# The chunk inverses of an RWKV-7 layer: 64x64 triangles doubled block by block, or two 32x32 diagonal blocks and a correction between them

## What is computed

```python
def step(S, inp):
    rt, wt, kt, vt, at, bt = inp
    sa = jnp.einsum('bhvk,bhk->bhv', S, at)
    S = S * wt[:, :, None, :] + sa[..., None] * bt[:, :, None, :] + vt[..., None] * kt[:, :, None, :]
    return S, jnp.einsum('bhvk,bhk->bhv', S, rt)
```

## Time and profile before

| | |
|---|---|
| three timed runs | 1850.35, 1838.9, 1853.22 us |
| span of the profiled execution | 1837.3 us |
| time of the profiled execution around its span | not given by the profile |
| the block's inverses, first mask of XT to last addition | 366.69 to 413.24 us |
| TensorE, VectorE, ScalarE busy over the span | 1732.0, 640.1, 345.0 us |

### The profile page before, as it was taken

One profiled execution on the slowest core, in us unless ns is written; L12 is line 12 of the kernel. 1 busy time (PEld: TensorE's weight loads), 2 busy tenths in 40 slices (PEclk: granted clock), 3 DMA queues, 4 the chain that ended last, 5 costly groups with the idle time before them and its releaser, 6 DMA issues.

```text
span 1837.3 us, 41974 instructions
## 1 busy us (share of the span) xinstructions
PE 1732.0 (94%) x19056; PEld 1137.2 (62%) x19056; DVE 640.1 (35%) x1196; ACT 345.0 (19%) x558; POOL 39.7 (2%) x49
## 2 busy tenths in 40 slices
PE   6989898789899999998999999999999999999994
PEld 6967565589899999996934435344353534447342
DVE  5534443674865544855632010120101002010021
ACT  3223231402443333534210000000000000000001
POOL 0010000000000000000000000000000000010100
PEclk9999999698999999999999999999999999999998
DMA  9130540200854443517499999999999999997995
GB/s 292 52 112 1 150 141 20 38 3 4 240 161 151 150 137 105 170 62 230 172 386 414 418 413 418 415 417 417 410 417 403 417 415 406 417 398 306 415 405 220
DMA packets 171303, 474.02 MB, mean 258 GB/s; under 512 B 28426, under 2 KB 114604, under 8 KB 140228
## 3 DMA queue, kind: packets, MB, share of 16 engines
q1 hardware_dynamic: 168574, 461.05, 66.3%
q0 software_dynamic: 2352, 10.23, 1.6%
q10 hardware_dynamic: 198, 0.05, 0.0%
HBM read 459.19 MB, written 15.24 MB: 258 GB/s over the span
## 4 chain that ended last, share of the span: by engine, by line
PE 47%; SPq 3%; DMA 2%; DVE 1%; issue 1%; ACT 0%; POOL 0%; POOLq 0%; ACTq 0%; DVEq 0%
PE bank L2662 43%; SPq L2321 2%; DMA ring<-in_moe_w_down 1%; PE bank L319 1%; PE bank L320 1%; PE bank L321 1%; SPq L2431 0%; SPq L2325 0%; PE bank L2513 0%; PE bank L2592 0%; PE bank L2636 0%; DMA ring<-y_rows_dram,y_index 0%; PE bank L2528 0%; PE bank L2547 0%; PE bank L2630 0%
## 5 line engine op out<-in xcount | busy, mean ns | idle before, releaser
L2662 PE MATMUL bank<-ring,x 128*32 128x512 f32 (+1 forms) x6144 | 587.3, 540 | 2.3 <-DMA ring<-in_moe_w_gu 2.0
L2662 PEld LDWEIGHTS bank<-ring,x 128*32 128x32 f32 x6144 | 203.9, 110 | 354.4 <-issue 333.7
L2662 PE MATMUL bank<-ring,hid 128*32 128x256 f32 x5376 | 292.1, 379 | 0.3 <-DMA ring<-in_moe_w_down 0.3
L2662 PEld LDWEIGHTS bank<-ring,hid 128*32 128x32 f32 x5376 | 184.4, 110 | 108.1 <-issue 2.3
L319 PE MATMUL bank<-x_hi,w_hi 128*128 128x320 f32 (+1 forms) x488 | 151.8, 311 | 0.0
L320 PE MATMUL bank<-x_lo,w_hi 128*128 128x320 f32 (+1 forms) x488 | 150.8, 309 | 0.0
L321 PE MATMUL bank<-x_hi,w_lo 128*128 128x320 f32 (+1 forms) x488 | 150.8, 309 | 0.0
L2130 DVE TENSOR_TENSOR w_lo<-ring,w_hi 128x2048 fp32r<-128x2048 f32 (+2 forms) x51 | 112.5, 2209 | 97.5 <-ACT w_hi L2052 97.2
L3015 DVE TENSOR_TENSOR hrow<-sil,bank 128x512 f32<-128x512 f32 (+1 forms) x48 | 26.9, 617 | 301.3 <-PE bank L2662 301.3
L2052 ACT ACTIVATE w_hi<-ring 128x2048 fp32r<-128x2048 f32 (+2 forms) x51 | 94.1, 1848 | 126.8 <-PE bank L321 124.2
L2787 ACT ACTIVATE sil<-bank 128x512 f32<-128x512 f32 (+1 forms) x48 | 22.7, 544 | 455.2 <-PE bank L2662 455.2
(11 more groups left out here) (576 smaller groups left out, 2122.8 us busy)
## 6 DMA issues: line engine op xcount, KB each, us to landing
ring<-in_moe_w_gu SPq DMA_DIRECT2D x128, 1024.0 KB
ring<-in_moe_w_down SPq DMA_DIRECT2D x112, 1024.0 KB
ring<-in_moe_w_gu SPq DMA_DIRECT2D x128, 768.0 KB
ring<-in_ffn_w_gu_even SPq DMA_DIRECT2D x44, 512.0 KB, 4.9
pages<-in_cache_mla SPq DMA_DIRECT2D x128, 144.0 KB, 2.5
ring<-in_w_in_odd SPq DMA_DIRECT2D x12, 1024.0 KB, 5.3
ring<-in_ffn_w_down_even SPq DMA_DIRECT2D x10, 1024.0 KB, 5.4
proj_ring<-in_w_in_even SPq DMA_DIRECT2D x9, 1024.0 KB
```

The lines of the kernel that those rows point to most:

```text
L2662: mm = t.matmul(ps[banks[g3]][SL * y:SL * y + SL, 0:w], act[:, g3, k, :], m_ring[:, slot, at + y * w:at + (y + 1) * w], start=start, stop= ...
```

## The change

The two diagonal 32x32 blocks of each 64x64 triangle are inverted first, in compact form, and the block that couples them comes in at the end:

- X, T1 and a new `XT_blocks` (XTb) are [128, 3, 8, 32]: the rows of a 32-row block hold that block's own 32 columns. `begin` takes them out of BM: rows of even blocks from columns 0 to 31, those of odd blocks from 32 to 63, by two masks and an addition. It has five operations where it had three.
- The levels 2 to 16 go through the same steps with 32x32 blocks: `level` has four matmuls per head on tiles 0 and 1 and two on tile 2, each 32 rows by 32 columns with 32 moving columns, in the four diagonal 32x32 tiles of the array. VectorE's operations have 256 elements for 512. Tile 2 leaves out its last update of X as before.
- Level 32 is replaced: a product of BM's off-diagonal block with X of the even blocks, which lands on the rows of the odd blocks; a copy into T1; a product of T1 and XTb, which lands on the rows of the even blocks; and an operation that adds this, on the even rows alone, to the right half of XT (`scalar_tensor_tensor`). Two products and two VectorE operations per tile, as before, but 16 matmuls each.
- ScalarE spreads XTb into the full XT: two activations per tile with a scale that is 1 on the rows of even or odd blocks and 0 elsewhere.
- The table of constants has 3804 columns for 3962.

```diff
--- before.py
+++ after.py
@@ -75,9 +75,13 @@
     s8T[:64, 64:128] = ((il // DS == jl // DS) & (il <= jl))[:64]
     f["sm_T"] = s8T
     f["ident64"] = il == jl
-    for s in (2, 4, 8, 16, 32):
-        f[f"lev{s}"] = (il // (2 * s) == jl // (2 * s)) & (il % (2 * s) >= s) & (jl % (2 * s) < s)
-    f["lev1_T"] = (il // 2 == jl // 2) & (jl % 2 >= 1) & (il % 2 < 1)
+    ib, jb = i % 32, p[None, 0:32]
+    for s in (2, 4, 8, 16):
+        f[f"lev{s}"] = (ib // (2 * s) == jb // (2 * s)) & (ib % (2 * s) >= s) & (jb % (2 * s) < s)
+    f["even32"], f["odd32"] = i // 32 % 2 == 0, i // 32 % 2 == 1
+    for half in ("even32", "odd32"):
+        f["lev1_" + half] = (ib // 2 == jb // 2) & (jb % 2 >= 1) & (ib % 2 < 1) & f[half]
+    f["ident32"] = ib == jb
     f["causal"] = np.where(i >= j, 0.0, -1e30)
 
     f["own"] = np.where((i % DS >= np.arange(DS)[None, :]), 0.0, -1e30)
@@ -1214,15 +1218,15 @@
                     KM = sbuf(rk, "KM", [P, 3, RH, 2, RC])
                     XT = sbuf(rk, "XT", [P, 3, RH, RC])
                     inv = rk.enter_context(ExitStack())
-                    X = sbuf(inv, "X", [P, 3, RH, RC])
-                    T1 = sbuf(inv, "T1", [P, 3, RH, RC])
+                    X, XTb, T1 = (sbuf(inv, n, [P, 3, RH, 32]) for n in ("X", "XT_blocks", "T1"))
                     pairs_full, pairs_ready, keys_full, keys_ready, xt_ready = (sem(x) for x in ("pairs_full", "pairs_ready", "keys_full", "keys_ready", "xt_ready"))
                     t_full, t_ready, d_full, d_ready = ([sem(f"{x}{i}") for i in range(3)] for x in ("t_full", "t_ready", "d_full", "d_ready"))
-                    LEVELS = [[2, 4, 8, 16, 32], [2, 4, 8, 16, 32], [2, 4]]
+                    LEVELS = [[2, 4, 8, 16], [2, 4, 8, 16], [2, 4]]
                     BLOCKS = [2, 2, 1]
+                    xt_spread = sem("xt_spread")
 
                     def heads(bank, r=P):
-                        return ps[bank][0:r, :].rearrange("p (h t) -> p h t", h=RH)
+                        return ps[bank][0:r, 0:RH * 32].rearrange("p (h t) -> p h t", h=RH)
                     ROWS = [rowB[:, 0, :], rowB[:, 1, :], rowK[:, 0, :], rowK[:, 1, :], rowB[:, 2, :]]
                     with nc.Block() as block:
                         @block.sync
@@ -1312,20 +1316,22 @@
                                 last.then_inc(ready, 1)
 
                             def over(name, r):
-                                return C(name, r).rearrange("p (o t) -> p o t", o=1).to_broadcast([r, RH, RC])
+                                return C(name, r).rearrange("p (o t) -> p o t", o=1).to_broadcast([r, RH, 32])
                             def begin(i):
                                 r = TILES[i][1]
                                 v.wait_ge(pairs_full, i + 1)
                                 masked(BM, i, (2 * i, 2 * i + 1), pairs_ready)
                                 v.wait_ge(pairs_ready, i + 1)
-                                dv(v, v.tensor_tensor(XT[0:r, i, :, :], BM[0:r, i, :, 0, :], over("lev1_T", r), ALU.mult))
-                                dv(v, v.tensor_tensor(XT[0:r, i, :, :], XT[0:r, i, :, :], over("ident64", r), ALU.add))
-                                v.transpose(X[0:r, i, :, :].rearrange("p h t -> p (h t)"), XT[0:r, i, :, :].rearrange("p h t -> p (h t)")).then_inc(xt_ready, 1)
+                                v.tensor_tensor(XTb[0:r, i, :, :], BM[0:r, i, :, 0, 0:32], over("lev1_even32", r), ALU.mult)
+                                dv(v, v.tensor_tensor(T1[0:r, i, :, :], BM[0:r, i, :, 0, 32:64], over("lev1_odd32", r), ALU.mult))
+                                dv(v, v.tensor_tensor(XTb[0:r, i, :, :], XTb[0:r, i, :, :], T1[0:r, i, :, :], ALU.add))
+                                dv(v, v.tensor_tensor(XTb[0:r, i, :, :], XTb[0:r, i, :, :], over("ident32", r), ALU.add))
+                                v.transpose(X[0:r, i, :, :].rearrange("p h t -> p (h t)"), XTb[0:r, i, :, :].rearrange("p h t -> p (h t)")).then_inc(xt_ready, 1)
                             v.wait_ge(st_full, NB)
                             v.wait_ge(stored.sem, stored.n)
                             begin(0)
                             begin(1)
-                            for li in range(5):
+                            for li in range(4):
                                 tiles = [i for i in range(3) if li < len(LEVELS[i])]
                                 for i in tiles:
                                     r = TILES[i][1]
@@ -1343,9 +1349,17 @@
                                         v.wait_ge(d_ready[i], li)
                                     else:
                                         v.wait_ge(xt_ready, i + 1)
-                                    if li < len(LEVELS[i]) - 1:
+                                    if i < 2 or li == 0:
                                         v.tensor_tensor(X[0:r, i, :, :], X[0:r, i, :, :], heads(2 * i + 1, r), ALU.add)
-                                    v.tensor_tensor(XT[0:r, i, :, :], XT[0:r, i, :, :], heads(2 * i, r), ALU.add).then_inc(d_ready[i], 1)
+                                    v.tensor_tensor(XTb[0:r, i, :, :], XTb[0:r, i, :, :], heads(2 * i, r), ALU.add).then_inc(d_ready[i], 1)
+                            for i in range(2):
+                                v.wait_ge(t_full[i], 5)
+                                v.tensor_copy(T1[:, i, :, :], heads(2 * i)).then_inc(t_ready[i], 1)
+                            for i in range(2):
+                                v.wait_ge(d_full[i], 5)
+                                v.wait_ge(xt_spread, i + 2)
+                                v.scalar_tensor_tensor(out=XT[:, i, :, 32:64], in0=heads(2 * i + 1), scalar=C("even32"), in1=XT[:, i, :, 32:64],
+                                                       op0=ALU.mult, op1=ALU.add).then_inc(d_ready[i], 1)
 
                         @block.scalar
                         def _(s):
@@ -1383,6 +1397,11 @@
                             for n in range(5):
                                 s.wait_ge(row_full, n + 1)
                                 s.activation(ROWS[n], ps[6 + n % 2][:, :], ACT.Copy).then_inc(row_act, 1)
+                            for i in (2, 0, 1):
+                                r = TILES[i][1]
+                                s.wait_ge(d_ready[i], len(LEVELS[i]))
+                                s.activation(XT[0:r, i, :, 0:32], XTb[0:r, i, :, :], ACT.Copy, scale=C("even32", r))
+                                s.activation(XT[0:r, i, :, 32:64], XTb[0:r, i, :, :], ACT.Copy, scale=C("odd32", r)).then_inc(xt_spread, 1)
 
                         @block.tensor
                         def _(t):
@@ -1455,11 +1474,16 @@
                                                           src[hs, pr, js], AR[hs, pr, :, js], start=True, stop=True)
                                 return mm
 
+                            def rows32(b):
+                                return slice(32 * b, 32 * b + 32)
+
+                            def cols32(h):
+                                return slice(32 * h, 32 * h + 32)
+
                             def level(i, bank, left, right):
                                 for h in range(RH):
-                                    for b in range(BLOCKS[i]):
-                                        js = slice(RC * b, RC * b + RC)
-                                        mm = t.matmul(ps[bank][js, h * RC:(h + 1) * RC], left(h, js), right(h, js), start=True, stop=True)
+                                    for b in range(2 * BLOCKS[i]):
+                                        mm = t.matmul(ps[bank][rows32(b), cols32(h)], left(h, b), right(h, rows32(b)), start=True, stop=True)
                                 return mm
 
                             t.wait_ge(ar_ready, 1)
@@ -1480,22 +1504,34 @@
                                         for q in range(2):
                                             mm = t.matmul(ps[6][64 * q:64 * q + 64, cols], bks[:, q, c, :], C("ident"), start=True, stop=True, tile_position=(0, 64 * q))
                                 mm.then_inc(row_full, 1)
-                            for li in range(5):
+                            for li in range(4):
                                 tiles = [i for i in range(3) if li < len(LEVELS[i])]
                                 for i in tiles:
                                     if li:
                                         t.wait_ge(d_ready[i], li)
                                     else:
                                         t.wait_ge(xt_ready, i + 1)
-                                    level(i, 2 * i, lambda h, js: BM[js, i, h, 0, :], lambda h, js: X[js, i, h, :]).then_inc(t_full[i], 1)
+                                    level(i, 2 * i, lambda h, b: BM[rows32(b), i, h, 0, cols32(b % 2)], lambda h, js: X[js, i, h, :]).then_inc(t_full[i], 1)
                                 if li < 3:
                                     t.wait_ge(*((keys_ready, li) if li else (row_act, 5)))
```

(18 more changed lines are left out.)

## The result

The changed kernel takes 1866.25 us, the median of 11 runs (1854.3 to 1873.61), against 1849.1 us for the kernel before in the same comparison (11 runs, 1837.89 to 1853.22). The ratio is 1.0103, 95% interval 1.0079 to 1.0126: slower by 1.0%, 14.6 to 23.3 us. The forecast was 1837.

The account below looks back on a forecast made before the run. TensorE was taken as the bound, with the block's gain reaching the end one to one. Level gains of 12.8 us and up to 0.2 for constants made 13, so 1850.35 - 13 = 1837 us; range 1827 to 1855.

Parts of the forecast that it names:

- What bounds the kernel, and that the block's length reaches the end: Whole kernel: TensorE, busy 94%, is the bound; no transfer sets the block's end, so its gain reaches the end one to one.
- The sum: Whole kernel: level gains of 12.8 us plus 0 to 0.2 for constants make 13, subtracted from the median 1850.35: 1837.
- A product's cost: Block's levels: a four-tile product of 64 pairs costs between 0.50 and 1.87 us, taken as 0.55; before, products were 0.93 apart.
- The 29 ns of before: Stretches longer than 2 us show no pair quicker than 29 ns, taken as the tiles' limit, not the supply's.
- My 31 ns for a record of 32x32: New products: from 110 and 58 ns for records 64 columns apart, 32 columns come to about 31 ns.
- Rival 2: TensorE's supply is worse than 19 ns a pair; at 29 ns the block ends 18 us later, 1868 us; chance 0.11.
- The clock: Block of the changed kernel: granted clock expected at 0.9 or more.
- rival 3: The clock falls as four 32x32 blocks half fill the array; levels 4 to 32 3 us slower, 1854 us; chance 0.13.
- VectorE: Block: operations on 256 elements take 0.41 us, each masking or update saves 0.27, a tile's start takes 2.0 us.
- The levels: Levels 2, 4, 8, 16, 32 gain 3.6, 2.6, 2.0, 2.6, 2.0 us; block 33.7 instead of 46.6, level 32 3.4.
- What a switch between tile shapes costs: Around the keys' pairs TensorE changes between 64-row and 32-row tiles six times, 0.2 us each, 1.2 in all.

Follow-up runs that it names:

- the last kernel: Kernel before with X by VectorE's transposition up to level 16, level 32 as off-diagonal products, keys' pairs ahead of tile 2's product: 1840.6 us, ratio 0.9969.
- half the count: Changed kernel with one matmul of 64 columns for two heads, using the first head's weights, so fewer pairs on the same tiles: 1845.2 us, ratio 0.9978.
- the wide left operands: Kernel with block-diagonal left operands in 64 columns, compact right operands with 32 columns moving, X by transposition, 64-row tiles: 1846.2 us, ratio 0.9985 to before.
- a kernel that doesn't stall: Kernel before with only the change's level 32, two off-diagonal products in 32-row tiles: 1846.4 us, ratio 0.9996.
- the halves: Kernel before with each 64x64 product matmul issued as two of 32 columns, same tiles and sums: 1925.5 us, ratio 1.0374.
- the transposition: X made by VectorE's 32x32 transposition instead of a product and an addition: in the changed kernel 1845.3 us, in the kernel before (up to level 16) 1845.2 us.

## Why the prediction was wrong

**What bounds the kernel, and that the block's length reaches the end: held.** 13.6 and 14.3 us more in the block, 17 us more in the median; 65 more gave 69, 76 more gave 76, 8 less gave 6 (the last kernel) and 5 (half the count), 5 less gave 2 (the wide left operands). The differences are within what the spread of the runs hides, and I leave them open. The sum was rightly taken from the median: the profiled execution of before was one of those that kept the full clock from 120 to 160 us. But "So no transfer is under way whose landing could set the end of the block" overlooked one kind: the 1% of load in the block was, by the view of transfers from 366.69 to 413.24 us, nothing but 10 packets of instructions, 9 of them on queue 8.

**A product's cost: this step failed.** "So a four-tile product costs between 0.50 and 64 x 29 ns = 1.87 us. I take 0.55, near the rows 439 and 1626, where tiles change as they will here." In a burst that was right: 8 ns a pair at 418.35. But those rows hold 45 and 4 matmuls, and a portion of instructions holds 128. Within a portion a row shows how fast TensorE reads what is there; only beyond it does it show how fast more arrives. From stall to stall a pair costs 28.5 ns (ten portions, 36.5 us), so a product of 64 costs 1.8 us, at my upper bound and more than three times my 0.55; over the whole block, with its waits, it is 30.9 ns, and 1950 pairs make 60.2 us. The rows bounded another quantity than the one that I needed. I had written that supply at no cost "is shown for 1 us only" and gave it a chance of 0.55 all the same.

**The 29 ns of before were read wrongly as well.** I took them for the time of 64 columns ("there the tiles set it"). With 32 columns they are 29 ns too, and they double with the clock, so the tile does set them but the moving columns don't. My 31 ns for a record of 32x32 came out of a difference of columns on 64-row tiles and agreed with the 8 ns a pair on four 32-row tiles by luck. That the supply's 28.5 ns lie so near these 29 hid the limit: the kernel before drew pairs about as fast as they can come, without one wait for issue among its products.

**The rival.** Rival 2 named the mechanism (supply worse than 19 ns a pair), with the decisive remark that the program holds twice the matmuls, and its far end, 29 ns, gave 1868 for the 1866.25 measured; its block end, 18 us later, was 4 too late, since the switches and short waits that I added (3.2 us) lie inside the stalls. That 1868 came so near is in part luck: the median rose by 3 us more than the block. It had a chance of 0.11 and lay outside the range. The bounds of the unknown cost were 0.50 and 1.87 us, and the range should have reached to what the upper one gives. By the 25 ns of the Trainium skill ("TensorE: Matmul & The Clock Gate", "Wait — 56ns, not 53.3ns?") the end would come 11 us later, near the truth, but not by its rule: starts are 8 to 14 ns apart here on four tiles and 1.7 us at the stalls. Gotcha 1 of the Trainium skill's "TensorEngine Tiling (Array Packing)", by which row tiles can't use one bank at the same time, doesn't hold here either: four row tiles write one bank at those 8 ns a pair.

**The clock.** I expected 0.9 or more, and it was 0.64. With the same tiles, 64 columns moving and half the count it stays at 0.90, so the half filled array of rival 3 doesn't bring it down by itself; of the kernels with 32-row tiles those that stall more have the lower clock (0.90, 0.73, 0.64, 0.54 for 4, 11, 18 and 40 us before issue). Which is the cause of which is not shown. It cost nothing that shows in the block, since a pair cost 31 ns at 0.54 as at 0.73.

**VectorE: held.** L1353 and L1354 take 0.42 and 0.41 us, a tile's start 2.1 us (376.09 to the masks at 378.17) for the 2.0 forecast, and VectorE's busy time in the block fell from 33.9 to 25.4 us. None of it shows in the time. **The levels:** with half the count the block took 37.98 us, 4.3 more than the 33.7 forecast, but that kernel still waited 4.3 us for issue, so whether the rest of the sum was right stays open; level 32, in a kernel that doesn't stall, took 3.9 us where I had 3.4. What a switch between tile shapes costs (0.2 us by my sum) was not measured by itself.

## What to carry to other kernels

A change that cuts TensorE's work into smaller matmuls has a price per instruction: count the pairs of load and matmul in the stretch and divide its length by them. Here a stretch at 28 to 31 ns a pair with waits for "issue" every 128 or 256 pairs was at the rate at which instructions arrive, and each further pair added that much. The figure alone doesn't tell: levels 4 to 16 of the kernel before come to 30 to 32 ns a pair by the pace of their tiles, without such a wait, and the halves stood at 59 ns and had no room either, since their tiles were full. A burst in the profile shows this limit only if it is longer than a portion of 128 pairs; the number of packets of the instruction queue in the stretch shows it too. At that limit an operation that an idle engine can do in place of a product (here the transposition) is worth the product's instructions, not its columns.

## What was unexpected of the hardware

- Instructions reach TensorE in packets of 16.4 KB, 256 instructions; in stretches that stall one comes per 3.5 to 4.0 us (3.65 to 3.8 on the mean), and TensorE stands still for 1.4 to 2.5 us at most of them; the pace was about the same at granted clocks of 0.54, 0.64 and 0.73.
- On 64-row tiles two side by side give one pair per 29 ns at full clock with 32 and with 64 columns moving, and one per 53 to 65 ns at half clock. On four 32-row tiles the columns do count: 8 ns a pair with 32 and 14 with 64 (in the kernel with half the count 32 records start within 0.45 us from 405.28 us on).
- Code that no edit touches lost some 10 us in one execution and none in the next, by half clock between 120 and 160 us.
